# The first matmul group behind a layer norm, issued chunk by chunk over four banks

## The chip, the cores and the metric

The kernel runs on one core of a Trainium2 chip. The metric is the device time of one execution in microseconds (us). The kernel before took 1475.57 us, the median of three runs from 1472.57 to 1479.77. Its profiled execution is a run of its own and took 1484.27 us.

## The reference, cut to what matters

One inference step of a decoder trunk with two layers, on 256 prompt tokens and 8 sample tokens (264 columns in the kernel), width 1024. In each layer a SwiGLU FFN, a token mixer and a second SwiGLU FFN follow one another, with a layer norm behind each:

```python
def swiglu(x, wg, wu, wd):
    return (jax.nn.silu(x @ wg) * (x @ wu)) @ wd

def decoder_layer(x, pos, lp, past):
    x = layer_norm(ALPHA * x + 0.5 * swiglu(x, lp['ffn_wg'][0], lp['ffn_wu'][0], lp['ffn_wd'][0]), lp['ln_g'][0], lp['ln_b'][0])
    y, st = token_mixing(x, pos, lp, past)
    x = layer_norm(ALPHA * x + y, lp['ln_g'][1], lp['ln_b'][1])
    x = layer_norm(ALPHA * x + 0.5 * swiglu(x, lp['ffn_wg'][1], lp['ffn_wu'][1], lp['ffn_wd'][1]), lp['ln_g'][2], lp['ln_b'][2])
    return x, st
```

So the work is one chain: six norms, and behind each but the last a product of the norm's whole output with new weights. The mixer begins with h @ w_in, whose columns feed three head groups; one of them also compresses old keys and values from cache pages (nsa_compress).

## The kernel before, in words

x lies with features on the partitions, in KC = 8 chunks of 128 x 264. A product in full precision is made of three matmuls on halves: every operand is split into a rounded high part and the low rest, and `product` (L713) issues low weight with high x (L715), high weight with low x (L716) and high weight with high x (L717). All are 128x128 weights on 264 columns, or on 512 columns in the mixer's projection.

An FFN's first part runs over 11 groups of weights of 256 hidden columns, gate and up, in three slots. Per group PE does two halves q, and for each a gate bank and an up bank with eight chunks of three matmuls: 96 matmuls on banks 0 to 3. Group n+1 reuses the banks of group n and waits for hidden_done, the multiplication on VectorE (DVE, L1522) that empties them behind the silu on ScalarE (ACT, L1195). In each group ACT splits the next group's weights (w_high, L1189, two halves), and DVE takes the rest of them (w_low, L1436), one half ahead of each silu and multiplication.

A norm ends like this: ACT writes x (L1168) and x_high or mix_x_high (L1170) per chunk; DVE writes the low part (L1418, or L1499 for the mixer) per chunk; the first bank of the next product waits for the low part of its chunk.

In the rows below the five places behind norms 0 to 4 are called M0 (mixer, first layer, near 230 us), F1 and F2 (FFN, near 530 and 742 us), M3 (mixer, second layer, near 954 us) and F3 (FFN, near 1253 us).

The mixer's product starts with four banks of 24 matmuls, whose readers are the convolution on DVE and the gelu on ACT, and goes on with four groups of three tiles on 512 columns (the projection). Between the tiles PE also compresses cache pages: `compress` (L637) needs a set of pages in bc_pages that SyncE's queue (SP, L435, four loads a set) has brought and DVE has weighted (L1581). There are two buffers; a set is loaded into one when the compression two sets earlier is done (bc_used). All orders are written out by hand, and each engine goes through its own list in order.

## Time and profile before

| | us |
|---|---|
| median of three runs | 1475.57 |
| profiled execution | 1484.27 |
| its span, first to last instruction | 1482.5 |
| TensorE busy | 1321.7 |
| VectorE busy | 815.5 |
| ScalarE busy | 516.0 |

The profile is of one execution. TensorE is the engine with most work, and the chain that ended last runs over it for 78% of the span. The mean clock granted to it is 0.926 of its full 2.4 GHz; it has two levels, full and half. Busy times overlap between engines, so what a stage costs is read from what its waits end on.

### The profile page before, as it was taken

The page shows a single profiled execution, that of the slowest core. Times are in us where ns is not written, and L with a number is a line of the kernel's source. Part 1 is how long each engine was busy: PE and PEld are TensorE (multiplying, and loading weights), DVE is VectorE, ACT ScalarE, POOL GpSimd, SP SyncE. Part 2 cuts the span into 40 slices and gives each one's busy share as a digit, 9 for nine tenths or more (in the row PEclk, how much of TensorE's full clock was granted, in tenths as well). Part 3 has the DMA queues.
Part 4 walks back from the last instruction along what each step waited for, and adds up shares of the span by engine and source line. Part 5 has one row for each costly group of instructions (what it writes and reads, how often), then busy time and mean ns, then how long its engine had stood idle before and what let it go on. Part 6 is the DMA issues. An engine that isn't in the chain of part 4 may idle for free.

```text
span 1482.5 us, 24841 instructions
## 1 busy us (share of the span) xinstructions
PE 1321.7 (89%) x9864; PEld 1165.0 (79%) x9864; DVE 815.5 (55%) x1548; ACT 516.0 (35%) x760; POOL 94.5 (6%) x160
## 2 busy tenths in 40 slices
PE   6999997996788979999899999798968787999994
PEld 5999996555565779999799999765646566999993
DVE  5565548764554365554465553678444653665433
ACT  3433335301334254333353333532122433434331
POOL 9000001001000010000110000100100001000001
PEclk9999998997679989999989999899867999999997
DMA  7654574457154235545635556544741713454530
GB/s 256 208 186 136 157 225 141 154 155 248 51 149 117 77 114 171 172 154 176 209 118 171 170 157 179 179 143 149 247 153 32 197 57 114 155 187 153 157 118 30
DMA packets 254824, 226.75 MB, mean 153 GB/s; under 512 B 12596, under 2 KB 234946, under 8 KB 254594
## 3 DMA queue, kind: packets, MB, share of 16 engines
q1 hardware_dynamic: 250530, 220.79, 47.3%
q0 software_dynamic: 4192, 4.56, 0.9%
q8 instruction: 69, 1.13, 0.3%
q14 instruction: 33, 0.27, 0.1%
HBM read 221.44 MB, written 3.86 MB: 152 GB/s over the span
## 4 chain that ended last, share of the span: by engine, by line
PE 78%; DVE 10%; SPq 3%; ACT 3%; issue 3%; DMA 2%; POOL 0%; DVEq 0%; ACTq 0%
PE bank L715 21%; PE bank L717 21%; PE bank L716 21%; PE bank L637 5%; PE bank L878 3%; PE bank L928 2%; SPq L403 1%; PE bank L724 1%; SPq L412 1%; PE bank L725 1%; DMA ring<-in_cache_a_kv_dram 1%; ACT x L1168 1%; DVE rstd L1737 1%; PE bank L1070 1%; PE bank L978 1%
## 5 line engine op out<-in xcount | busy, mean ns | idle before, releaser
L715 PE MATMUL bank<-x_high,w_low 128*128 128x264 f32 x1408 | 406.6, 289 | 28.4 <-DVE x_low L1418 24.4
L716 PE MATMUL bank<-x_low,w_high 128*128 128x264 f32 x1408 | 403.6, 287 | 0.0
L717 PE MATMUL bank<-x_high,w_high 128*128 128x264 f32 x1408 | 403.4, 287 | 0.0
L1436 DVE TENSOR_TENSOR w_low<-weights,w_high 128x2048 fp32r<-128x2048 f32 (+1 forms) x172 | 347.7, 2039 | 68.8 <-ACT w_high L1147 53.7
L715 PEld LDWEIGHTS bank<-x_high,w_low 128*128 128x128 f32 x1408 | 269.7, 192 | 32.3 <-issue 27.9
L716 PEld LDWEIGHTS bank<-x_low,w_high 128*128 128x128 f32 x1408 | 270.4, 192 | 0.0
L717 PEld LDWEIGHTS bank<-x_high,w_high 128*128 128x128 f32 x1408 | 268.8, 191 | 0.0
L715 PE MATMUL bank<-hidden_high,w_low 128*128 128x264 f32 x704 | 205.0, 291 | 0.0
L717 PE MATMUL bank<-hidden_high,w_high 128*128 128x264 f32 x704 | 199.9, 284 | 0.0
L716 PE MATMUL bank<-hidden_low,w_high 128*128 128x264 f32 x704 | 198.9, 283 | 0.0
L1189 ACT ACTIVATE w_high<-weights 128x2048 fp32r<-128x2048 f32 (+1 forms) x88 | 163.8, 1861 | 6.2 <-DMA weights<-in_ffn_wu_dram 6.1
L1522 DVE TENSOR_TENSOR shared<-shared,bank 128x264 f32<-128x264 f32 x88 | 37.8, 429 | 192.5 <-PE bank L717 192.5
L1195 ACT ACTIVATE shared<-bank 128x264 f32<-128x264 f32 x88 | 34.4, 391 | 300.8 <-PE bank L717 300.8
L1147 ACT ACTIVATE w_high<-weights 128x1408 fp32r<-128x1408 f32 (+1 forms) x84 | 125.6, 1543 | 28.9 <-DMA weights<-in_w_in_dram 28.9
L715 PEld LDWEIGHTS bank<-hidden_high,w_low 128*128 128x128 f32 x704 | 132.5, 188 | 0.8
L716 PEld LDWEIGHTS bank<-hidden_low,w_high 128*128 128x128 f32 x704 | 132.4, 188 | 0.8
L717 PEld LDWEIGHTS bank<-hidden_high,w_high 128*128 128x128 f32 x704 | 132.6, 188 | 0.0
L561 POOL TENSOR_TENSOR z<-z,mean_sb 128x264 f32<-128x264 f32 x45 | 36.6, 846 | 1158.2 <-DVE mean_sb L1472 1158.2
L1157 ACT ACTIVATE ring<-z 128x264 f32<-128x264 f32 x48 | 20.3, 424 | 248.0 <-DVE z L1470 248.0
L1470 DVE SCALAR_TENSOR_TENSOR z<-bank,x 128x264 f32<-128x264 f32 x48 | 20.7, 432 | 149.2 <-PE bank L717 105.6
L715 PE MATMUL bank<-w_high,mix_x_low 128*128 128x512 f32 (+1 forms) x192 | 78.7, 410 | 0.0
L716 PE MATMUL bank<-w_low,mix_x_high 128*128 128x512 f32 (+1 forms) x192 | 77.0, 401 | 0.0
(307 smaller groups left out, 1733.1 us busy)
## 6 DMA issues: line engine op xcount, KB each, us to landing
weights<-in_ffn_wg_dram SPq DMA_DIRECT2D x44, 1024.0 KB, 5.1
weights<-in_ffn_wu_dram SPq DMA_DIRECT2D x44, 1024.0 KB, 7.4
weights<-in_ffn_wd_dram SPq DMA_DIRECT2D x64, 704.0 KB, 5.8
weights<-in_w_in_dram SPq DMA_DIRECT2D x20, 1024.0 KB, 5.1
bc_pages<-in_cache_bc_kv_dram SPq DMA_DIRECT2D x128, 128.0 KB, 2.1
ring<-in_cache_bs_kv_dram SPq DMA_DIRECT2D x96, 128.0 KB, 2.2
ring<-in_cache_bw_kv_dram SPq DMA_DIRECT2D x12, 512.0 KB, 4.0
weights<-in_cache_bs_kv_dram SPq DMA_DIRECT2D x32, 128.0 KB, 3.6
```

Of the source, the lines that this page charges most:

```text
L561: nc.gpsimd.tensor_tensor(z[:, c, :], z[:, c, :], mean_sb[:, :], ALU.subtract).then_inc(sub_done, 1)
L637: return mm(*a, skip_group_check=True, **k)
L715: mm(out, w_low, v_high, start=start, stop=False)
L716: mm(out, w_high, v_low, start=False, stop=False)
L717: return mm(out, w_high, v_high, start=False, stop=stop)
L878: last = mm(out, w[:, c, (g % 4) * P:(g % 4 + 1) * P], mixed[:, c, :], start=(c == 0), stop=(c == KC - 1))
L928: last = nc.tensor.transpose(out[:, j * P:(j + 1) * P], tile, ident)
L1147: go(high(k, half), raw(k, half), ACT.Copy).then_inc(high_done, 1)
L1189: go(high(k, q), raw(k, q), ACT.Copy).then_inc(high_done, 1)
L1195: go(silu[:, q, :], banks[2 * q][:, 0:TOK], ACT.Silu).then_inc(silu_done, 1)
L1436: tt(low(k, half), raw(k, half), high(k, half).bitcast(F32), ALU.subtract).then_inc(low_done, 1)
L1522: tt(h, h, banks[2 * q + 1][:, 0:TOK], ALU.mult).then_inc(hidden_done, 1)
```

## The change

In the FFNs behind a norm (all but the first of the program) the first group is issued by a new function `opening`: the chunks are the outer loop, the four banks the inner one. `product` takes its matmuls in another order, so that the one with x_low comes last, and can be told to wait ahead of that one. The mixer's first four banks are issued in the same way, and their three compressions stand together behind them. For the mixer's norms ACT writes mix_x_high ahead of x, and DVE's low part waits for both. In the first group of these FFNs ACT splits both halves of the next weights ahead of the two silus, and DVE both low halves ahead of the two multiplications.

```diff
@@ -674,14 +674,36 @@
                                 pe.wait_ge(low_done, done + (i + 1))
                             wh, wl = (w(k, i).rearrange("p (c f) -> p c f", c=KC) for w in (high, low))
                             for c in range(KC):
-                                if isinstance(n0, int) and n0 + q + i == 0:
+                                if f == 0 and isinstance(n0, int) and n0 + q + i == 0:
                                     pe.wait_ge(low_x_ready, (3 * l + 2 * j) * KC + c + 1)
                                 last = product(banks[2 * q + i][:, 0:TOK], wh[:, c, q * P:(q + 1) * P],
                                                wl[:, c, q * P:(q + 1) * P], x_high[:, c, :], x_low[:, c, :],
                                                c == 0, c == KC - 1)
                             last.then_inc(full, 1)
 
-                for g in range(SLOTS):
+                def opening(k):
+
+                    pe.wait_ge(hidden_done, f * FC)
+                    pe.wait_ge(low_done, halves_before(l, k) + 2)
+                    halves = [[w(k, i).rearrange("p (c f) -> p c f", c=KC) for w in (high, low)] for i in range(2)]
+                    n = 3 * l + 2 * j - 1
+                    for c in range(KC):
+                        pe.wait_ge(high_x_ready, n * KC + c + 1)
+                        low_ready = (low_x_ready, (n + 1) * KC + c + 1)
+                        for q in range(2):
+                            for (wh, wl), full in zip(halves, (gate_full, up_full)):
+                                last = product(banks[2 * q + (full is up_full)][:, 0:TOK], wh[:, c, q * P:(q + 1) * P],
+                                               wl[:, c, q * P:(q + 1) * P], x_high[:, c, :], x_low[:, c, :],
+                                               c == 0, c == KC - 1, low_ready)
+                                low_ready = None
+                                if c == KC - 1:
+                                    last.then_inc(full, 1)
+
+                if f:
+                    opening(base)
+                else:
+                    group(base, halves_before(l, base), 0)
+                for g in range(1, SLOTS):
                     group(base + g, halves_before(l, base + g), 2 * g)
                 with pe.Fori(1, LOOPED) as i:
                     for s in range(SLOTS):
@@ -709,12 +731,13 @@
 
                 residual(3 * l + 2 * j, down)
 
-            def product(out, w_high, w_low, v_high, v_low, start, stop):
-
+            def product(out, w_high, w_low, v_high, v_low, start, stop, low_ready=None):
 
                 mm(out, w_low, v_high, start=start, stop=False)
-                mm(out, w_high, v_low, start=False, stop=False)
-                return mm(out, w_high, v_high, start=False, stop=stop)
+                mm(out, w_high, v_high, start=False, stop=False)
+                if low_ready is not None:
+                    pe.wait_ge(*low_ready)
+                return mm(out, w_high, v_low, start=False, stop=stop)
 
             def residual(n, y_chunk):
 
@@ -757,16 +780,17 @@
 
 
                 k = WIN_USE
-                for m in range(4):
-                    out = bank_v() if m < 2 else bank_a()
-                    for c in range(KC):
-                        if m == 0:
-                            pe.wait_ge(low_x_ready, (3 * l + 1) * KC + c + 1)
-                        last = product(out[:, 0:TOK], *parts_of(k, c, slice(m * P, (m + 1) * P)),
-                                       mix_x_high[:, c, :], mix_x_low[:, c, :], c == 0, c == KC - 1)
-                    last.then_inc(v_full if m < 2 else a_full, 1)
-                    if m:
-                        compress()
+                outs_f = [bank_v(), bank_v(), bank_a(), bank_a()]
+                for c in range(KC):
+                    pe.wait_ge(high_x_ready, 3 * l * KC + c + 1)
+                    for m in range(4):
+                        last = product(outs_f[m][:, 0:TOK], *parts_of(k, c, slice(m * P, (m + 1) * P)),
+                                       mix_x_high[:, c, :], mix_x_low[:, c, :], c == 0, c == KC - 1,
+                                       None if m else (low_x_ready, (3 * l + 1) * KC + c + 1))
+                        if c == KC - 1:
+                            last.then_inc(v_full if m < 2 else a_full, 1)
+                for m in range(3):
+                    compress()
 
                 for g in range(4):
                     k = WIN_USE + 1 + g
@@ -1165,9 +1189,11 @@
                     act.wait_ge(norm_done, n * KC + c + 1)
                     affine = dict(bias=params[:, l, 24 + i * 8 + c:25 + i * 8 + c],
                                   scale=params[:, l, i * 8 + c:i * 8 + c + 1])
+                    if i == 0:
+                        go(mix_x_high[:, c, :], z[:, c, :], ACT.Identity, **affine).then_inc(high_x_ready, 1)
                     go(x[:, c, :], z[:, c, :], ACT.Identity, **affine).then_inc(x_ready, 1)
-                    if split_x(n):
-                        go((x_high if i else mix_x_high)[:, c, :], z[:, c, :], ACT.Identity, **affine).then_inc(high_x_ready, 1)
+                    if i and split_x(n):
+                        go(x_high[:, c, :], z[:, c, :], ACT.Identity, **affine).then_inc(high_x_ready, 1)
                 if i != 0 and n < 3 * DEPTH - 1:
 
                     go(warm[:, :], warm[:, :], ACT.Silu)
@@ -1182,11 +1208,15 @@
                 def group(g, i=None):
 
                     k = base + g + 1
+                    value = landed_value(l, k)
+                    act.wait_ge(landed[k % SLOTS], value if i is None else i * 32 + value)
+                    opened = f and g == 0 and i is None
+                    if opened:
+                        for q in range(2):
+                            go(high(k, q), raw(k, q), ACT.Copy).then_inc(high_done, 1)
                     for q in range(2):
-                        if q == 0:
-                            value = landed_value(l, k)
-                            act.wait_ge(landed[k % SLOTS], value if i is None else i * 32 + value)
-                        go(high(k, q), raw(k, q), ACT.Copy).then_inc(high_done, 1)
+                        if not opened:
+                            go(high(k, q), raw(k, q), ACT.Copy).then_inc(high_done, 1)
                         n = f * FC + 2 * g + q
                         act.wait_ge(gate_full, n + 1 if i is None else i * (2 * SLOTS) + (n + 1))
                         if i is not None or n >= 2:
@@ -1493,6 +1523,7 @@
             def low_of_norm(n, c):
 
                 dve.wait_ge(high_x_ready, n * KC + c + 1)
+                dve.wait_ge(x_ready, (n + 1) * KC + c + 1)
                 if n % 3:
                     low_x(c)
                 else:
@@ -1507,8 +1538,12 @@
 
                 def group(g, i=None):
 
+                    opened = f and g == 0 and i is None
+                    if opened:
+                        split_low(l, base + g + 1)
                     for q in range(2):
-                        split_low(l, base + g + 1, (q,), i)
+                        if not opened:
+                            split_low(l, base + g + 1, (q,), i)
                         n = 2 * g + q
                         value = f * FC + n + 1
                         if i is not None:
```

PE, at the start of the FFN behind norm 1; L715 to L717 are the three matmuls of a product. Before:

```order
L715 MATMUL bank<-x_high,w_low 128x264 [waits low_done,low_x_ready,hidden_done,v_free]
L716 MATMUL bank<-x_low,w_high 128x264
L717 MATMUL bank<-x_high,w_high 128x264
L715 MATMUL bank<-x_high,w_low 128x264 [waits low_x_ready]
L716 MATMUL bank<-x_low,w_high 128x264
L717 MATMUL bank<-x_high,w_high 128x264
```

After, with L736, L737 and L740 in their place:

```order
L736 MATMUL bank<-x_high,w_low 128x264 [waits low_done,high_x_ready,hidden_done,v_free]
L737 MATMUL bank<-x_high,w_high 128x264
L740 MATMUL bank<-x_low,w_high 128x264 [waits low_x_ready]
L736 MATMUL bank<-x_high,w_low 128x264
L737 MATMUL bank<-x_high,w_high 128x264
L740 MATMUL bank<-x_low,w_high 128x264
L736 MATMUL bank<-x_high,w_low 128x264
L737 MATMUL bank<-x_high,w_high 128x264
```

The wait for x_low moved from the first matmul of a chunk to the third, and further banks follow before the next chunk.

PE, in the mixer behind norm 0, around the compressions (L637). Before, the end of the second bank, the first compression and the third bank's start:

```order
L716 MATMUL bank<-mix_x_low,w_high 128x264
L717 MATMUL bank<-mix_x_high,w_high 128x264
L637 MATMUL bank<-bc_pages,consts 32x256 [waits bc_weighted]
L637 MATMUL bank<-bc_pages,consts 32x256 x3
L715 MATMUL bank<-mix_x_high,w_low 128x264 [waits low_done]
```

After, the end of the four banks, and then the projection's first matmuls:

```order
L740 MATMUL bank<-mix_x_low,w_high 128x264
L637 MATMUL bank<-bc_pages,consts 32x256 [waits bc_weighted]
L637 MATMUL bank<-bc_pages,consts 32x256 x3
L637 MATMUL bank<-bc_pages,consts 32x256 [waits bc_weighted]
L637 MATMUL bank<-bc_pages,consts 32x256 x3
L637 MATMUL bank<-bc_pages,consts 32x256 [waits bc_weighted]
L637 MATMUL bank<-bc_pages,consts 32x256 x3
L736 MATMUL bank<-w_high,mix_x_low 128x512 [waits low_done,v_free]
L737 MATMUL bank<-w_high,mix_x_high 128x512
```

The three compressions, which had 24 matmuls between them, now stand side by side ahead of the projection.

DVE, in the first group of the FFN behind norm 1: w_low is the low half of weights, L1522 the multiplication. Before:

```order
L1436 TENSOR_TENSOR w_low<-weights,w_high 128x2048 [waits high_done,states_stored,rows_stored]
L1522 TENSOR_TENSOR shared<-shared,bank 128x264 [waits up_full,silu_done]
L1524 CAST hidden_high<-shared 128x264 [waits hidden_done]
L1526 TENSOR_TENSOR hidden_low<-shared,hidden_high 128x264 [waits hidden_high_done]
L1436 TENSOR_TENSOR w_low<-weights,w_high 128x2048 [waits high_done]
L1522 TENSOR_TENSOR shared<-shared,bank 128x264 [waits up_full,silu_done]
```

After, with L1466 for the split and L1557 for the multiplication:

```order
L1466 TENSOR_TENSOR w_low<-weights,w_high 128x2048 [waits high_done,states_stored,rows_stored]
L1466 TENSOR_TENSOR w_low<-weights,w_high 128x2048 [waits high_done]
L1557 TENSOR_TENSOR shared<-shared,bank 128x264 [waits up_full,silu_done]
L1559 CAST hidden_high<-shared 128x264 [waits hidden_done]
L1561 TENSOR_TENSOR hidden_low<-shared,hidden_high 128x264 [waits hidden_high_done]
L1557 TENSOR_TENSOR shared<-shared,bank 128x264 [waits up_full,silu_done]
```

The second half's split moved ahead of the first multiplication.

## Rows read from the trace of the kernel before

**Rows 1.** The page: the span, and the busy time of each engine.

```profile
span 1482.5 us, 24841 instructions
...
PE 1321.7 (89%) x9864; PEld 1165.0 (79%) x9864; DVE 815.5 (55%) x1548; ACT 516.0 (35%) x760; POOL 94.5 (6%) x160
```

**Rows 2.** PE's waits: us in total, times, longest us.

```profile
PE bank L715 <- DVE x_low L1418: 24.4, 8, 7.5
PE bank L715 <- issue: 19.1, 3, 7.5
```

**Rows 3.** Timeline of ACT at F1: start us, us, instruction [idle before].

```profile
527.65 0.61 ACT L1168 ACTIVATE x<-z,params 128x264 f32<-128x264 f32 x1 [2.56 <-DVE z L1486]
...
535.17 0.59 ACT L1170 ACTIVATE x_high<-z,params 128x264 fp32r<-128x264 f32 x1
535.78 1.28 ACT L1173 ACT_TABLE_LOAD   x1
...
537.18 1.89 ACT L1189 ACTIVATE w_high<-weights 128x2048 fp32r<-128x2048 f32 x1
```

**Rows 4.** Timeline of DVE at F1.

```profile
529.31 0.97 DVE L1418 TENSOR_TENSOR x_low<-x,x_high 128x264 fp32r<-128x264 f32 x1
...
539.21 2.29 DVE L1436 TENSOR_TENSOR w_low<-weights,w_high 128x2048 fp32r<-128x2048 f32 x1 [2.98 <-ACT w_high L1189]
541.47 0.43 DVE L1522 TENSOR_TENSOR shared<-shared,bank 128x264 f32<-128x264 f32 x1
```

**Rows 5.** Timeline of PE at F1.

```profile
530.43 0.56 PE L715 MATMUL bank<-x_high,w_low 128*128 128x264 f32 x1 [7.54 <-DVE x_low L1418]
...
536.63 0.39 PE L717 MATMUL bank<-x_high,w_high 128*128 128x264 f32 x1
536.82 0.42 PE L715 MATMUL bank<-x_high,w_low 128*128 128x264 f32 x1
...
540.10 0.29 PE L715 MATMUL bank<-x_high,w_low 128*128 128x264 f32 x1
540.23 0.29 PE L716 MATMUL bank<-x_low,w_high 128*128 128x264 f32 x1
```

**Rows 6.** Stretches: us, busy us of each engine (instructions), PEclk, DMA, GB/s.

```profile
530.40:547.10 16.70, 15.57 (x97) 14.79 (x98) 9.98 (x17) 12.92 (x18) 0.00 (x0) 0.81 0.00 1
...
742.20:758.90 16.70, 16.69 (x97) 15.70 (x98) 10.00 (x17) 12.90 (x18) 3.67 (x8) 0.72 0.03 9
...
954.00:972.90 18.90, 18.88 (x121) 16.25 (x121) 14.21 (x27) 11.20 (x17) 0.00 (x0) 0.75 0.18 53
...
1252.80:1268.00 15.20, 14.54 (x98) 13.69 (x99) 9.92 (x17) 12.92 (x18) 0.00 (x0) 0.87 0.00 1
310.50:313.40 2.90, 0.00 (x0) 0.00 (x1) 2.68 (x8) 0.00 (x0) 0.00 (x0) 1.00 0.55 150
313.40:318.20 4.80, 4.80 (x20) 3.48 (x21) 1.49 (x2) 0.00 (x0) 2.05 (x4) 0.64 0.65 189
```

**Rows 7.** Timelines of PE, SP and DVE at M0.

```profile
241.12 0.64 PE L637 MATMUL bank<-bc_pages,consts 128*32 128x256 f32 x8
...
248.47 0.64 PE L637 MATMUL bank<-bc_pages,consts 128*32 128x256 f32 x8
...
241.96 10.18 SPq L435 DMA_DIRECT2D bc_pages<-in_cache_bc_kv_dram  x12
...
246.07 1.22 DVE L1581 TENSOR_TENSOR bc_pages<-bc_pages,cmp_w 128x1024 f32<-128x1024 f32 x1 [2.26 <-DMA bc_pages<-in_cache_bc_kv_dram]
```

**Rows 8.** Timelines of PE and DVE at M3.

```profile
964.91 0.64 PE L637 MATMUL bank<-bc_pages,consts 128*32 128x256 f32 x8
...
972.26 0.64 PE L637 MATMUL bank<-bc_pages,consts 128*32 128x256 f32 x8
...
970.71 1.23 DVE L1581 TENSOR_TENSOR bc_pages<-bc_pages,cmp_w 128x1024 f32<-128x1024 f32 x1 [3.20 <-DMA bc_pages<-in_cache_bc_kv_dram]
```

**Rows 9.** The page: DMA issues, KB each, us to landing.

```profile
bc_pages<-in_cache_bc_kv_dram SPq DMA_DIRECT2D x128, 128.0 KB, 2.1
```

## The prediction

> **What bounds the kernel now.** I read the page first. The tensor engine (PE) is busy for 1321.7 of 1482.5 us [rows 1], so a gain has to come out of its idle stretches or out of the clock it is granted. Next I read the list of what PE waits for. Two lines concern the matmuls on a norm's output: 24.4 us for x_low and 19.1 us put down to "issue", the longest of both 7.5 us [rows 2]. There are five such places, one behind each norm but the last. I call them F1, F2, F3 (the norm hands over to an FFN; near 530, 742 and 1253 us) and M0, M3 (to the mixer; near 230 and 954 us). The timelines of ACT, DVE and PE at F1 show the handover. ACT makes x and x_high chunk by chunk, about 1.0 us per chunk, from 527.65 to 535.76, loads a table and starts on the next weights at 537.18 [rows 3]. DVE makes x_low(0) at 529.31 [rows 4]. PE starts at 530.43, and until 536.63 it has done only 24 matmuls, since its first bank takes three per chunk; then the other 72 of the group run freely [rows 5].
>
> The second thing to see is the clock. Fifteen matmuls from 536.82 to 540.10 go by at 0.219 us each; from 540.10 on one takes 0.12 us [rows 5]: 1.2 GHz and 2.4 GHz. The table by stretches gives the share granted. From a share s over a length L the time at half speed is 2(1-s)L, and half of that is lost: F1 6.3 us (3.2 lost), F2 9.4 (4.7), F3 4.0 (2.0), M3 9.5 (4.7) [rows 6]. The clock is low because PE had just been idle for 7.5 us. After 2.9 us of idleness, from 310.5 to 313.4, the next 4.8 us also had a share of only 0.64 [rows 6], so a wait of 3 us suffices.
>
> **The change, part by part.**
>
> *Opening of an FFN.* The same 96 matmuls are issued in another order: twelve per chunk on four banks. Only the third of the twelve needs x_low first, and the later chunks arrive every 1.0 us while twelve matmuls take 12 x 0.12 = 1.45 us or 12 x 0.219 = 2.6 us. So PE never waits again after x_low(0). Two of the 96 are done before it. The other 94 take, with h us at half speed, h + (94 - h/0.219) x 0.12 = 11.3 + 0.45h. For h under gapless work I take 4 us (F3's 4.0 and the 3.5 behind 313.4 [rows 6]), with 2.8 to 6.3 as bounds: 13.1 us (12.5 to 14.1), so F1 would end at 530.4 + 13.1 = 543.5.
>
> What is late next is DVE. PE's second group reuses the first two banks, and waits until the multiplication that empties them is done. In the old order the banks were full 48 matmuls earlier, and this was hidden. Now the four banks get full within the last 12 matmuls, and DVE has put both low halves ahead of that multiplication. Its chain from ACT: first w_high starts at 537.18, DVE's first w_low at 539.21, its end at 541.47 [rows 3, 4]; the second adds 2.26 (543.7) and the multiplication 0.43 and some 0.1 for the handover: 544.3. That is later than 543.5, and sets the start of group two. Before it was 547.1, so -2.8 at F1. The same 13.9 us behind the first matmul gives 756.1 instead of 758.9 at F2 (-2.8), and 1266.7 instead of 1268.0 at F3 (-1.3) [rows 6]. PE idles for about 0.8 us in there; that is less than the 2.9 above, and I charge no loss of clock. Splitting both halves first costs ACT nothing: it had been ahead of PE anyway. Group two itself has its weights split by then, and what it frees, it frees earlier.
>
> *Opening of the mixer.* Here the order also moves three compressions (L637). They stood behind the second, third and fourth bank; now all three stand behind the last matmul. bc_pages has two buffers. The third compression needs a set of pages which SP may load only when the first compression is done, and which DVE then weights. The rows of M0: first compression 241.12 to 241.76, loads issued from 241.96, DVE starts at 246.07 and needs 1.22, so 5.5 us from the one's end to the other's start. At M3 964.91 + 0.64 to 970.71 + 1.23: 6.4 us [rows 7, 8]. In between PE had 48 matmuls and a compression; now it has one compression of 0.6 us. So a new wait of about 4.9 and 5.8 us stands in PE's queue, and behind it the whole projection. Working M3 out: opening 954.0 + 13.1 = 967.1, first compression 0.64, reload 6.4, third 0.64: 974.8, against 972.26 + 0.64 = 972.9 before: +1.9. At M0 the reload is 0.9 shorter: +1.0. The wait is longer than the 2.9 us that lowered the clock, so the projection starts at half speed; with the 4 us from above that loses 2.0 (1.4 to 3.2). Together +3.0 and +3.9. x_high ahead of x (norms 0 and 3) lets two matmuls go earlier and leaves x_low where it was: nothing. The later product order issues as many matmuls and weight loads as before: nothing. DVE's additional wait is for an x that ACT wrote just ahead of, or 0.5 us behind, x_high: nothing.
>
> The Trainium skill speaks against this piece. "DMA: Bandwidth & Descriptors", section Rules for kernel authors, tells to issue a DMA early, compute, and wait late, since the fixed cost then overlaps; the moved compressions take that computing away. The same page (Anatomy of one DMA) fits the fixed cost at about 2.0 us on the GpSimd path. Estimated by that page a reload would be 2.0 + 1.2 = 3.2 us, and the sum would be 5.5 us lower; the rows of this kernel say 5.5 and 6.4, and I go by them.
>
> **Sum.** Against the profiled execution (1484.27 us, of which 1482.5 is span): -2.8 - 2.8 - 1.3 + 3.0 + 3.9 = 0. But that execution is 8.7 us above the median of the runs (1475.57), and in four of five openings its clock came late. In an execution where it comes as early as at F3, the old opening loses less while the new one, bound by DVE or by the reload, gains nothing from it. So for the runs I take F nearer F3: -1.7 each (between -1.0 and -2.8), -5.1 in all. For M an early clock gives the old opening up to (9.5 - 4.0)/2 = 2.8 back, so between +3.0 and +6.7; I take +4.8 each, +9.6. Net +4.5: 1480.
>
> **Rivals.**
> 1. *The half clock behind the reload lasts.* In the projection PE shares its time with waits for bc_pages, so the clock may need as long as at M3 and F2 (9.5 us, 4.7 lost) instead of 4. For: four of five openings show 6 us and more. Against: the projection's matmuls come gapless. It adds 2.7 to each M: +4.5 + 5.4 = +9.9, 1485.5, slower. It decides from about 6.9 us at half speed on.
> 2. *The reload is quick.* The list of DMA issues has 2.1 us from issue to landing for one load of bc_pages [rows 9]; if the four of a set overlapped, the reload would be 2.1 + 1.2 = 3.3, the wait 2.7 us, below the one that lowered the clock. Each M then falls by 2.2 to 3.1 and by the 2.0 of clock: +0.1 each at most, -5 to -8 in all with the F: 1469, the side of faster. Against: 4.1 us in M0's own rows.
> 3. *The delay is absorbed.* Later in the mixer PE waits for caches. If those loads were not held up by the compressions, the M would cost nothing: -5, 1470.5. Against: SP issues the caches behind the page loads in one queue.
> 4. *Changing banks costs.* The Trainium skill's "TensorE: Matmul & The Clock Gate", section A second HAM failure mode, tells of micro-idles when a kernel cycles through banks, which lower the clock. As a mechanism here: all 94 matmuls at 0.219 = 20.6 us, F +4 each, M +7.5 more each, about +35: 1510. Against: the one bank change in the rows, 536.63 to 536.82, has a step of 0.19, no gap [rows 5].
>
> **Chances.** Forecast 0.58 (within 0.5% 0.50, slower 0.08), rival 1 0.22 (slower 0.20, within 0.02), rival 2 0.13 (faster 0.08, within 0.05), rival 3 0.05 (faster 0.02, within 0.03), rival 4 0.02 (slower). A measurement of this kernel can tell about 0.5% (7.4 us) from no change. That makes faster 0.10, same 0.60, slower 0.30. The bounds: F 3 x (-2.8 to -1.0) and M 2 x (+3.0 to +6.7) give -2.4 to +10.4; the runs scatter by 3 to 4 us; so 1471 to 1488.
>
> **What would show it.** Right: at F1 to F3 no wait of PE between x_low(0) and the end of the opening; DVE's second w_low ending after PE's opening, with PE idle for up to 1 us; group two 13.9 us behind the first matmul that needs x_low. In the mixer: PE idle 5 to 6 us ahead of the third compression, released by DVE's weighting, and a share of 0.5 behind it. Wrong: a third compression without a wait (rivals 2, 3), gaps inside the opening (rival 4), or a second group that starts at PE's own pace.

## The result, and the profile after

The changed kernel takes 1482.40 us (median of 20 runs, 1474.73 to 1490.76), the kernel before 1477.81 (20 runs, 1469.01 to 1484.46). The ratio is 1.0045, with a 95% interval from 1.0027 to 1.0063: slower by 4 to 9 us (6.7 by the ratio; the medians are 4.6 apart). The profiled execution has a span of 1481.0 us, against 1482.5 in [rows 1]; as single executions scatter by more than the change, the stages have to be read one by one.

The page of the changed kernel, the lines that answer to [rows 1]:

```profile
span 1481.0 us, 24880 instructions
...
PE 1312.8 (89%) x9864; PEld 1159.1 (78%) x9864; DVE 815.1 (55%) x1548; ACT 516.6 (35%) x760; POOL 94.8 (6%) x160
```

What PE of the changed kernel waits for (us in total, times, longest), answering to [rows 2]:

```profile
PE bank L637 <- DVE bc_pages L1616: 20.6, 8, 5.2
PE bank L736 <- ACT x_high L1196: 18.0, 3, 6.0
...
PE bank L736 <- ACT mix_x_high L1193: 11.3, 2, 5.6
```

The 7.5 us behind each norm became 6.0 and 5.6, and they end on the high half now. The compressions' waits for bc_pages are 20.6 us in eight now, the longest 5.2. Both are what the change does by its order; what they are worth is in the timelines.

PE at F1 in the changed kernel, where [rows 5] stood:

```profile
527.75 0.56 PE L736 MATMUL bank<-x_high,w_low 128*128 128x264 f32 x1 [6.01 <-ACT x_high L1196]
528.10 0.42 PE L737 MATMUL bank<-x_high,w_high 128*128 128x264 f32 x1
529.20 0.59 PE L740 MATMUL bank<-x_low,w_high 128*128 128x264 f32 x1 [0.68 <-DVE x_low L1448]
...
542.34 0.28 PE L740 MATMUL bank<-x_low,w_high 128*128 128x264 f32 x1
542.97 0.39 PE L736 MATMUL bank<-x_high,w_low 128*128 128x264 f32 x1 [0.35 <-DVE shared L1557]
```

DVE there, where [rows 4] stood:

```profile
538.08 4.49 DVE L1466 TENSOR_TENSOR w_low<-weights,w_high 128x2048 fp32r<-128x2048 f32 x2 [2.99 <-ACT w_high L1216]
542.49 0.42 DVE L1557 TENSOR_TENSOR shared<-shared,bank 128x264 f32<-128x264 f32 x1
```

From the first matmul on x_low to group two PE takes 13.8 us (529.20 to 542.97), without a gap until the last, and the row at 542.97 names DVE's multiplication, which follows the two splits at once.

PE at M0 in the changed kernel, where [rows 7] stood:

```profile
244.47 1.07 PE L637 MATMUL bank<-bc_pages,consts 128*32 128x256 f32 x16
250.74 1.08 PE L637 MATMUL bank<-bc_pages,consts 128*32 128x256 f32 x8 [5.20 <-DVE bc_pages L1616]
```

The first row is two compressions, the second the third one: it waits 5.2 us, and itself takes 1.08 us, where a compression took 0.64. The reload of its set, on SP's queue and on DVE:

```profile
245.31 10.14 SPq L435 DMA_DIRECT2D bc_pages<-in_cache_bc_kv_dram  x12
...
249.46 1.23 DVE L1616 TENSOR_TENSOR bc_pages<-bc_pages,cmp_w 128x1024 f32<-128x1024 f32 x1 [4.89 <-DMA bc_pages<-in_cache_bc_kv_dram]
```

The set's four loads are the first of the twelve in SP's row. In the trace SP issues them one after another, from 245.31 to 247.47, and the last lands at 249.43, 2.0 us behind its issue; DVE, idle for 4.9 us, starts at once.

The changed kernel by stretches (columns as in [rows 6]): projection's first tile at M0 and M3, and the openings F1, F2 and F3 from the first matmul on x_low:

```profile
251.80:259.70 7.90, 7.90 (x27) 6.02 (x24) 5.03 (x14) 0.00 (x0) 0.00 (x0) 0.70 0.59 187
529.20:543.00 13.80, 13.44 (x95) 13.24 (x95) 9.32 (x16) 11.62 (x18) 0.00 (x0) 0.86 0.01 1
738.40:752.10 13.70, 12.94 (x94) 12.73 (x94) 9.22 (x15) 11.95 (x18) 3.72 (x8) 0.90 0.04 11
...
968.80:976.60 7.80, 7.80 (x28) 5.96 (x24) 5.11 (x15) 0.00 (x0) 0.00 (x0) 0.71 0.61 202
1252.60:1266.40 13.80, 13.53 (x95) 13.32 (x95) 9.32 (x16) 11.53 (x18) 0.00 (x0) 0.85 0.01 1
```

The three FFN openings take 13.7 to 13.8 us, where 16.7, 16.7 and 15.2 stood (counted there from the first matmul, which waited for the first x_low). The projection's first tile of 24 matmuls takes 7.8 to 7.9 us with a share of 0.70 and 0.71.

The clock falls a second time later in the mixer. The seventh tile, from the seventh compression to the eighth, at M0, in the kernel before and in the changed one:

```profile
277.57:283.88 6.31, 6.31 (x32) 4.58 (x32) 4.86 (x7) 2.10 (x4) 0.00 (x0) 1.00 0.32 88
...
282.52:290.43 7.91, 7.91 (x32) 5.74 (x32) 4.87 (x7) 2.10 (x4) 0.00 (x0) 0.78 0.42 115
```

To compare places across kernels I count from the start of DVE's copy of a norm's mean. "Group three" is the 193rd matmul of an FFN, "first tile done" the start of the fourth compression, "twelfth compression done" the start of the matmul behind it.

| us behind the mean | before | changed | FFN part alone | mixer part alone | compressions inside | all three moves | filled norms |
|---|---|---|---|---|---|---|---|
| M0 projection starts | 26.4 | 28.9 | 24.9 | 28.9 | 25.1 | 23.2 | 22.5 |
| M0 first tile done | 32.1 | 36.9 | 30.6 | 36.8 | 31.0 | 29.4 | 29.5 |
| M3 first tile done | 32.0 | 36.6 | 30.6 | 36.6 | 30.7 | 29.1 | 28.9 |
| M0 twelfth compression done | 87.4 | 93.8 | 85.9 | 93.7 | 86.3 | 86.3 | 86.3 |
| M3 twelfth compression done | 87.4 | 93.4 | 85.9 | 93.5 | 86.0 | 84.4 | 84.2 |
| F1 group two | 24.1 | 21.2 | 21.5 | 24.1 | 21.2 | 21.7 | 19.0 |
| F1 group three | 35.7 | 32.9 | 33.3 | 35.7 | 32.9 | 33.5 | 30.8 |
| F2 group three | 35.8 | 32.9 | 32.9 | 35.5 | 32.9 | 32.8 | 32.4 |
| F3 group three | 34.1 | 32.9 | 32.9 | 34.1 | 33.7 | 33.4 | 30.8 |

In the two traces the FFNs give back 2.8, 2.9 and 1.2 us. The mixers cost 4.8 and 4.6 up to the end of the first tile, and 6.4 and 6.1 up to the end of the twelfth compression, since the seventh tile takes 7.9 us instead of 6.3 or 6.4. A wait of 1.7 us for bc_pages stands ahead of that tile in all 24 mixers of the twelve kernels traced here, the kernel before among them. The clock falls behind it in all six in which PE stood idle for 5.2 to 5.3 us ahead of the third compression (changed kernel, mixer part alone, x first), and in two of the 18 others (M0 of all three moves and of the filled norms). Why it falls there is open. Further on single executions differ by more than this: from one norm's mean to the next M0's mixer takes 300.3 us before and 299.0 after, M3's 298.7 and 305.1.

### The profile page after: what moved, and what is told of

Its sections match the earlier page's. It is cut to its first block, busy times and chain, and to the rows that moved or that the text cites. A ratio compares the mean times of both kernels' runs of the same rounds, so it can differ in the third digit from the quotient of the medians.

```text
span 1481.0 us, 24880 instructions
## 1 busy us (share of the span) xinstructions
PE 1312.8 (89%) x9864; PEld 1159.1 (78%) x9864; DVE 815.1 (55%) x1548; ACT 516.6 (35%) x760; POOL 94.8 (6%) x160
## 4 chain that ended last, share of the span: by engine, by line
PE 75%; DVE 11%; ACT 5%; SPq 4%; issue 2%; DMA 2%; POOL 0%; DVEq 0%; ACTq 0%
PE bank L736 20%; PE bank L737 20%; PE bank L740 20%; PE bank L637 5%; PE bank L902 3%; PE bank L952 2%; SPq L403 2%; DVE w_low L1466 1%; PE bank L747 1%; SPq L412 1%; PE bank L748 1%; DMA ring<-in_cache_a_kv_dram 1%; ACT x L1194 1%; PE bank L937 1%; ACT x_high L1196 1%
## 5 line engine op out<-in xcount | busy, mean ns | idle before, releaser
L736 PE MATMUL bank<-x_high,w_low 128*128 128x264 f32 x1408 | 404.1, 287 | 23.5 <-ACT x_high L1196 18.0
L740 PE MATMUL bank<-x_low,w_high 128*128 128x264 f32 x1408 | 402.5, 286 | 2.0 <-DVE x_low L1448 2.0
L737 PE MATMUL bank<-x_high,w_high 128*128 128x264 f32 x1408 | 402.5, 286 | 0.0
L1466 DVE TENSOR_TENSOR w_low<-weights,w_high 128x2048 fp32r<-128x2048 f32 (+1 forms) x172 | 347.5, 2039 | 69.5 <-ACT w_high L1171 53.8
L736 PEld LDWEIGHTS bank<-x_high,w_low 128*128 128x128 f32 x1408 | 268.9, 191 | 25.3 <-issue 23.3
L740 PEld LDWEIGHTS bank<-x_low,w_high 128*128 128x128 f32 x1408 | 267.5, 190 | 3.0 <-DVE x_low L1448 3.0
L737 PEld LDWEIGHTS bank<-x_high,w_high 128*128 128x128 f32 x1408 | 269.1, 191 | 0.0
L736 PE MATMUL bank<-hidden_high,w_low 128*128 128x264 f32 x704 | 204.1, 290 | 0.0
L737 PE MATMUL bank<-hidden_high,w_high 128*128 128x264 f32 x704 | 200.5, 285 | 0.0
L740 PE MATMUL bank<-hidden_low,w_high 128*128 128x264 f32 x704 | 200.0, 284 | 0.0
L1219 ACT ACTIVATE w_high<-weights 128x2048 fp32r<-128x2048 f32 (+1 forms) x82 | 152.4, 1858 | 6.8 <-DMA weights<-in_ffn_wu_dram 6.7
L1557 DVE TENSOR_TENSOR shared<-shared,bank 128x264 f32<-128x264 f32 x88 | 37.7, 428 | 185.6 <-PE bank L740 185.6
L736 PEld LDWEIGHTS bank<-hidden_high,w_low 128*128 128x128 f32 x704 | 132.8, 189 | 0.8
L737 PEld LDWEIGHTS bank<-hidden_high,w_high 128*128 128x128 f32 x704 | 132.3, 188 | 0.8
L740 PEld LDWEIGHTS bank<-hidden_low,w_high 128*128 128x128 f32 x704 | 132.3, 188 | 0.0
L736 PE MATMUL bank<-w_high,mix_x_low 128*128 128x512 f32 (+1 forms) x192 | 82.1, 428 | 0.0
L737 PE MATMUL bank<-w_high,mix_x_high 128*128 128x512 f32 (+1 forms) x192 | 80.0, 417 | 0.0
```

Source lines behind the costliest of these rows:

```text
L736: mm(out, w_low, v_high, start=start, stop=False)
L737: mm(out, w_high, v_high, start=False, stop=False)
L740: return mm(out, w_high, v_low, start=False, stop=stop)
L1219: go(high(k, q), raw(k, q), ACT.Copy).then_inc(high_done, 1)
L1466: tt(low(k, half), raw(k, half), high(k, half).bitcast(F32), ALU.subtract).then_inc(low_done, 1)
L1557: tt(h, h, banks[2 * q + 1][:, 0:TOK], ALU.mult).then_inc(hidden_done, 1)
```

## The experiments

**FFN part alone.** The mixer's opening goes back to bank by bank:

```diff
-                for c in range(KC):
-                    pe.wait_ge(high_x_ready, 3 * l * KC + c + 1)
-                    for m in range(4):
-                        ...
-                for m in range(3):
-                    compress()
+                for m in range(4):
+                    for c in range(KC):
+                        ...
+                    if m:
+                        compress()
```

> The changed kernel with the mixer's first four banks in the old order again (bank by bank, a compression behind each of the last three); the FFN openings stay as changed. My theory (the FFN openings gain, the mixer's loses more): no wait of 5 us ahead of the third compression, 249.1 - 230.1 = 19 us again from the first matmul on x_low to the projection, group two of the FFNs still 13.8 us behind the first matmul on x_low. Time 5 us under the kernel before (ratio 0.9966, between 0.994 and 0.999). Rival (the FFN openings do not matter, or cost): ratio 1.000 or above. Rival (the loss lies in the FFN openings): ratio 1.004, like the whole change.

Measured: 1470.73 us, ratio 0.9952 (0.9928 to 0.9975), 7 us under the kernel before. The long wait for bc_pages is gone, and the FFNs keep their gain (2.4, 2.9 and 1.2 us up to group three). Not all of the 7 us need be theirs: in this trace the mixers are 1.5 us shorter than before too, as the clock rose earlier in their opening (at M0 a share of 0.88 from 229.6 to 246.6 us, against 0.75 from 230.5 to 249.1 before). The rivals, that the FFN openings do not matter or cost, fall.

**Mixer part alone.** PE's `opening` is not called (ACT and DVE split no half ahead either, which is not shown):

```diff
-                if f:
-                    opening(base)
-                else:
-                    group(base, halves_before(l, base), 0)
+                group(base, halves_before(l, base), 0)
```

> The changed kernel with the first group of the FFNs in the old order again, and the weights' halves split one by one; the mixer's opening stays as changed. My theory: the wait of 5.2 us ahead of the third compression and the half clock behind it stay, nothing is gained at the FFNs: 9 to 10 us over the kernel before (ratio 1.006, between 1.003 and 1.009). Rival (the mixer's wait is absorbed later by the waits for caches): ratio 1.000. Rival (the loss lies in the FFNs): ratio 1.000 or below.

Measured: 1489.01 us, ratio 1.0082 (1.0050 to 1.0113), 12 us over the kernel before by the ratio, 11 by the medians. PE at M0 of this version:

```profile
244.15 1.07 PE L637 MATMUL bank<-bc_pages,consts 128*32 128x256 f32 x16
250.47 1.08 PE L637 MATMUL bank<-bc_pages,consts 128*32 128x256 f32 x8 [5.25 <-DVE bc_pages L1613]
```

The same wait as in the whole change, and no later wait absorbs it: by the end of the twelfth compression M0 is 6.3 and M3 6.1 us behind the kernel before. By the ratios the two parts, -7.1 and +12.1, add up to +5.0, and the whole measured +6.7; by the medians -7.2 and +11.1 make +4.0, and the whole +4.6. That fits within the intervals.

**Compressions inside the opening.** The first behind the fourth chunk, the second behind the sixth, the third at the end:

```diff
+                    if c in (3, 5):
+                        compress()
-                for m in range(3):
-                    compress()
+                compress()
```

> The changed kernel with the first compression behind the fourth chunk of the mixer's opening, the second behind the sixth, the third behind the last; all else as changed. My theory: the reload of 5.5 to 6.4 us now runs beside the last four chunks, the wait ahead of the third compression falls from 5.2 us to under 1, the clock stays at full speed into the projection: each mixer gains 5 to 8 us on the changed kernel, total 10 to 15 us under it and 5 to 10 us under the kernel before (ratio 0.994 to 0.997). Rival (the wait is not the reload, but DVE's order of work): the wait stays at 4 us or more, ratio 1.004.

Measured: 1465.94 us, ratio 0.9935 (0.9908 to 0.9962). PE's compressions at M0:

```profile
238.79 0.64 PE L637 MATMUL bank<-bc_pages,consts 128*32 128x256 f32 x8
...
242.47 0.64 PE L637 MATMUL bank<-bc_pages,consts 128*32 128x256 f32 x8
...
247.40 0.64 PE L637 MATMUL bank<-bc_pages,consts 128*32 128x256 f32 x8 [1.21 <-DVE bc_pages L1617]
```

DVE at the same place:

```profile
245.15 0.42 DVE L1626 COPY shared<-bank 128x256 f32<-128x256 f32 x1 [2.00 <-PE bank L740]
...
246.12 1.22 DVE L1617 TENSOR_TENSOR bc_pages<-bc_pages,cmp_w 128x1024 f32<-128x1024 f32 x1
```

The wait fell from 5.2 to 1.2 us. What is left is the rival's share: DVE copies the first banks before it weights the third set, and these copies wait for the opening's end. The reload itself is hidden, and the loss has become a gain: up to the end of the twelfth compression each mixer is 7.4 to 7.5 us shorter than in the changed kernel. The ratio is a little better than the range expected.

**Filling the wait.** Between the second and the third compression, in the changed kernel:

```diff
                 for m in range(3):
+                    if m == 2:
+                        for _ in range(11):
+                            mm(banks[5][:, 0:256], mean_w, consts[:, 0:256], start=True, stop=True, skip_group_check=True)
                     compress()
```

> The changed kernel with 11 matmuls that nobody reads (fp32, 256 columns, some 0.45 us each, 4.9 us in all) between the second and the third compression, into a bank that is free there; they fill the wait of 5.2 us without shortening it. If the half clock behind the wait is a cost of its own (my theory): the share granted stays 1.0 from the opening's rise into the projection, the projection's first tile is 2 to 3 us shorter, 4 to 6 us under the changed kernel in all (ratio to the kernel before 1.000 to 1.002). If the wait alone is the cost (rival): no shorter than the changed kernel, ratio 1.0045.

Measured: 1477.60 us, ratio 1.0003 (0.9977 to 1.0029). Its stretches at M0, from the first compression to the projection, and the first tile:

```profile
243.20:251.20 8.00, 6.53 (x47) 4.64 (x46) 1.86 (x5) 5.35 (x5) 0.00 (x0) 1.00 0.45 123
251.20:257.20 6.00, 5.88 (x32) 4.47 (x30) 5.63 (x16) 0.00 (x0) 0.00 (x0) 1.00 0.61 170
```

The clock stays at 1.00 and the first tile takes 5.9 us, although the third compression starts no sooner (28.7 and 28.0 us behind the mean, in the changed kernel 27.9 and 27.8). The second fall is gone too. So the half clock is a cost of its own: 1.7 and 2.1 us up to the end of the first tile, 3.3 and 3.6 up to the end of the twelfth compression, about half of the loss. Its interval just touches that of the whole change, so it is the two shares, 0.70 and 1.00, and the tile's 7.9 and 5.9 us that show it more than the time.

**All three moves.** The version with the compressions inside, and on DVE the first multiplication back between the two low halves, and the third weighting ahead of the copies:

```diff
-                    opened = f and g == 0 and i is None
-                    if opened:
-                        split_low(l, base + g + 1)
                     for q in range(2):
-                        if not opened:
-                            split_low(l, base + g + 1, (q,), i)
+                        split_low(l, base + g + 1, (q,), i)
                 ...
+                weight()
                 for c in range(2):
                     ...
-                weight()
```

> The version with the compressions inside the mixer's opening, and two more moves on DVE: in the FFNs' first group the second low half stands behind the first multiplication again (ACT still splits both halves ahead of the silus), and in the mixer the third set of pages is weighted ahead of the copies that wait for the opening's end. My theory: DVE's second split is what holds group two of the FFNs, so it now starts within 0.6 us of the end of the opening, 0.5 to 1 us earlier at each; the 1.2 us wait ahead of the third compression is DVE's order and goes. In all 3 to 5 us less than the version with the compressions inside alone, ratio to the kernel before 0.991. Rival: the split is needed for the up bank of group two, whose wait takes what is gained: no difference at the FFNs, ratio 0.992 to 0.994.

Measured: 1467.41 us, ratio 0.9946 (0.9922 to 0.9971), not to be told from the compressions inside alone. In the trace both mixers are 1.6 us shorter again up to the first tile's end, and the third compression does not wait; at M0 the second fall of the clock takes this back. The FFNs are not shorter: group two follows the opening without a gap, but two of the openings (F1, F2) took longer, since the clock rose later. The time did not bear out the 3 to 5 us.

**Halves one by one.** The version with the compressions inside, and ACT and DVE in the old order beside PE's new opening, a single run. On ACT, and on DVE as in the version above:

```diff
-                    opened = f and g == 0 and i is None
+                    opened = False
```

> The version with the compressions inside the opening, but ACT and DVE split the next weights' halves one by one again, as in the kernel before, while PE keeps the new opening. My theory: the second high half then waits behind the first silu for the end of the opening, the second low half behind it, and PE waits for it in the up bank of group two: a gap of 1 to 2 us inside group two, group three starts 0.5 to 1.5 us later than 32.9 us behind the norm's mean. Rival (splitting ahead is not needed): no gap, group three at 32.9 us or earlier.

PE at F1 of this version, the only gap inside group two:

```profile
544.27 0.39 PE L736 MATMUL bank<-x_high,w_low 128*128 128x264 f32 x1 [0.48 <-DVE w_low L1467]
```

PE waits for the second low half, as expected, though for 0.5 us and not 1 to 2. At F2 and F3 the wait is 0.5 us too. Group two takes 12.5 us at all three FFNs, in the version above, which differs on ACT alone in the FFNs, 11.8: splitting ahead on ACT is worth 0.6 to 0.7 us. Group three starts at 33.4, 34.2 and 34.0 us, 0.5 to 1.3 later than in the changed kernel, but the rest of that is the opening, which ended 0.2 to 1.4 us later here. The single run's 1470.33 us says nothing at this size.

**Filling the norms of the kernel before.** Behind the statistics of five norms:

```diff
                 stats(KC - 1)
+                if n < 3 * DEPTH - 1:
+                    for _ in range(16):
+                        mm(banks[5][:, 0:256], mean_w, consts[:, 0:256], start=True, stop=True, skip_group_check=True)
```

> The kernel before with 16 matmuls that nobody reads (fp32, 256 columns, some 0.43 us each, 6.9 us in all) behind the statistics of each of the first five norms, in a stretch in which PE was idle for 7.5 us; nothing is shortened by them. If the half clock at the openings costs what the table by stretches says (my theory): the share granted stays 1.0 through the norms, each opening is 1.5 to 3 us shorter, the mixers' 4 us, 12 us in all: ratio 0.990 to 0.994. If the openings are bound by the order of their work and not by the clock (rival): ratio 0.999 to 1.001.

Measured: 1473.24 us, ratio 1.0007 (0.9990 to 1.0024): no change, which is the rival's forecast and not mine. The stretches F1 and F2, from the first matmul on x_low to group two:

```profile
521.20:537.50 16.30, 14.83 (x97) 13.36 (x97) 9.71 (x17) 12.71 (x18) 0.00 (x0) 0.90 0.00 1
732.90:747.70 14.80, 13.32 (x96) 11.86 (x96) 9.70 (x16) 12.69 (x18) 3.48 (x7) 1.00 0.03 10
```

With a full clock F2 took 15.0 us from its first matmul (732.70 to 747.72) instead of 16.7, and at F1 the clock fell in the middle all the same. In the old opening the first bank goes at the pace at which ACT and DVE hand over the chunks: at F2 it takes 6.3 us at full clock (732.70 to 739.02) with waits of up to 0.37 us for x_low, and 6.7 us at half clock in the kernel before (742.21 to 748.89). Most of the gain is in the other three banks. In this trace F2 and M3 start their next stage 1.6 and 1.5 us earlier than in the profiled execution before, M0, F1 and F3 within 0.1 us of it.

**Filled norms.** All three moves, the first two compressions behind the fifth and seventh chunk, and 12 such matmuls behind each of the five norms:

```diff
+                if n < 3 * DEPTH - 1:
+                    for _ in range(12):
+                        mm(banks[5][:, 0:256], ...)
-                    if c in (3, 5):
+                    if c in (4, 6):
```

> The version with all three moves, the first two compressions behind the fifth and seventh chunk, and 12 matmuls that nobody reads behind each of the first five norms (5.2 us of the 5.6 to 6.0 in which PE is idle there). My theory: the openings run at full speed, 94 matmuls in 11.5 us; group two of the FFNs starts near 19.5 us behind the mean instead of 21.2, the mixers' projection near 21.5 instead of 25: 8 to 13 us under the version without the filling, ratio to the kernel before 0.982 to 0.987. Rival (DVE's splits bound the FFNs whatever the clock): the FFNs unchanged, the mixers alone gain, ratio 0.987 to 0.990.

Measured: 1460.81 us, ratio 0.9915 (0.9887 to 0.9943). By the median this is the fastest version, 14 us under the kernel before in the same series and 6.6 under all three moves; the intervals of the three versions with the compressions inside overlap. The gain over the version without the filling is under the 8 to 13 us expected. F1, from the first matmul on x_low to group two:

```profile
525.10:536.70 11.60, 11.59 (x95) 11.51 (x95) 7.11 (x15) 11.14 (x17) 0.00 (x0) 1.00 0.01 1
```

95 matmuls in 11.6 us at F1, and F3 is like it; at F2 the clock fell once and group two started at 20.6 us. The mixers gained less than expected: the tile ahead of the fourth compression now ends in a wait of 1.2 us for that compression's pages, and at M0 the clock fell again in the seventh tile (7.9 us).

**Filled norms, halves split ahead.** The same, with both low halves ahead of the first multiplication again, a single run:

```diff
+                    opened = f and g == 0 and i is None
+                    if opened:
+                        split_low(l, base + g + 1)
                     for q in range(2):
-                        split_low(l, base + g + 1, (q,), i)
+                        if not opened:
+                            split_low(l, base + g + 1, (q,), i)
```

> The version with the filled norms, with DVE's two low halves ahead of the first multiplication again, as in the changed kernel. My theory: with PE at full speed the opening ends 19 us behind the mean, but the multiplication cannot begin before 20.7 us, so group two starts at 21.2 us at all three FFNs whatever the clock, with PE idle for 2 us; the version with the multiplication between the halves started it at 19.0. Rival (DVE does not decide): group two at 19.0 again.

DVE at F1 of this version:

```profile
527.45 4.49 DVE L1470 TENSOR_TENSOR w_low<-weights,w_high 128x2048 fp32r<-128x2048 f32 x2 [2.99 <-ACT w_high L1220]
531.87 0.42 DVE L1561 TENSOR_TENSOR shared<-shared,bank 128x264 f32<-128x264 f32 x1
```

PE's group two there:

```profile
532.34 0.39 PE L736 MATMUL bank<-x_high,w_low 128*128 128x264 f32 x1 [2.06 <-DVE shared L1561]
```

Group two starts at 21.2 us at all three FFNs. PE is idle for 2.1 us before it at F1 and F2, and for 0.5 at F3, where the clock fell in the opening (a share of 0.87). Without the split ahead it started at 19.0, 20.6 and 19.0. So DVE's order decides here, and the clock that PE had does not.

**x first.** The changed kernel with x ahead of mix_x_high in the mixers' norms, a single run:

```diff
+                    go(x[:, c, :], z[:, c, :], ACT.Identity, **affine).then_inc(x_ready, 1)
                     ...
-                    go(x[:, c, :], z[:, c, :], ACT.Identity, **affine).then_inc(x_ready, 1)
```

> The changed kernel with ACT writing x ahead of mix_x_high again in the mixers' norms. My theory: the first matmul of the mixer's opening is 0.5 us later, the first one on the low half and all behind it where they were (7.4 us behind the mean, projection at 28.8 to 28.9): no effect on the time. Rival: the opening starts later as a whole, by 0.5 us.

The first matmul moved from 5.6 to 6.1 us behind the mean; the first on x_low (7.4) and the projection (28.7 and 28.8) stayed. The single run's 1487.95 us says nothing at this size.

## Why the prediction was right

The predicted time was 1480.0 with 1471 to 1488; measured were 1482.4. Of the 2.4 us between them 2.2 are the kernel before, whose median of 20 runs is 1477.81 where three runs gave 1475.57. The change itself was put at +4.5 and measured +4.6 by the medians, +6.7 by the ratio. The mechanism was right; that the sum is so near is partly luck, as both of its terms were too small and have opposite signs.

- **The FFN opening** held to its size. Predicted were 13.9 us from the first matmul on x_low to group two, measured 13.7 to 13.8 three times; -2.8, -2.8 and -1.3 against the profiled execution, measured -2.8, -2.9 and -1.2. For the runs I took -5.1; the part alone measured -7.1 (-10.6 to -3.7).
- **What is late next** is DVE, as the step said. The changed kernel's own row names it, and with a full clock the start stays at 21.2 us until the multiplication moves. Where the clock rose later, PE itself was as late: at F1 of the FFN part alone group two starts at 21.5 without a wait.
- **The reload** is the new wait: 5.2 us twice, against 4.9 and 5.8 predicted. Filling it, removing it and the part alone all point to it. Rival 2 (a quick reload) falls: one load lands in 2.0 to 2.2 us, but SP issues the four over 2.2 us, so they overlap only in part. Rival 3 (absorbed later) falls, as the loss is still there at the twelfth compression and in the part's time. The Trainium skill's rule ("DMA: Bandwidth & Descriptors", Rules for kernel authors: issue early, compute, wait late) is borne out by the compressions inside, which is that rule applied. The 2.0 us that the Trainium skill ("DMA: Bandwidth & Descriptors", Anatomy of one DMA) gives for one DMA on the GpSimd path are near what one of these loads takes on SP. The estimate with them was too short, since it left out the time between the issues: DVE starts 4.2 us behind the first (245.31 to 249.46).
- **The mixer's size** was too small against the profiled execution: +3.0 and +3.9 predicted, +4.8 and +4.6 measured at the end of the first tile. The opening took 14.0 to 14.3 us instead of 13.1, as its clock rose later than the 4 us I took; the third compression took 1.08 us instead of 0.64, a term I had left out; and the tile behind it lost 2.1 to 2.2 us instead of 2.0. At M3 the reload was some 0.7 us shorter than I had it. The second fall of the clock, another 1.5 to 1.6 us at each mixer, I had not foreseen at all.
- **The step to the runs** came out for a weak reason. I gave the old mixer's opening up to 2.8 us back for an early clock, from the rule that half of the time at half speed is lost. The filled norms of the kernel before show that this overstates it: 4.7 us were "lost" at F2, and a full clock gave 1.7 back. The +4.8 per mixer that I took is what the first tile shows, but for another reason, and the part alone measured +12.1 for two (+7.4 to +16.7), near the 6.4 and 6.1 of the trace at the twelfth compression.
- **Rival 1** (the half clock behind the reload lasts) did not come in its form: a share of 0.70 over 7.9 us is 4.7 us at half speed, and the clock was full again within 8 us. Part of its price came all the same: the seventh tile, a share of 0.78 over 7.9 us, adds 3.5 us at half speed, together 8.2, above the 6.9 from which it would decide. **Rival 4** (changing banks costs) did not come: with a full clock the opening's 95 matmuls took 11.6 us, PE busy for 11.59 of them.
- **"A wait of 3 us suffices"** was read from one row and does not hold everywhere. In the version with the compressions inside PE waits 2.91 us for bc_pages at M3 (until 1022.93), and the 5 us behind it have a share of 1.00.

## What to carry to other kernels

When a loop is turned inside out, look at everything that was spread over it: the compressions waited for nothing between the banks and for 5 us side by side, because a reload with two buffers ran beside the matmuls. And when all banks fill at the same time, the engine that empties them must not have long work queued ahead; what was 48 matmuls of slack becomes a wait. Here the wait of 5.2 us on PE was paid more than once: as itself, in the tile behind it (2.1 to 2.2 us), and in a tile 30 us later (1.5 to 1.6 us). But a share of half clock is only worth what the stretch would gain from a faster PE.

## What was not expected of the hardware

Matmuls that nobody reads, put where PE had waited for 5.2 us, kept the clock at 1.00, and the tile behind them took 5.9 us instead of 7.9. Behind the norms, with an order of work that can use it, they brought the openings of F1 and F3 from 14.3 and 14.2 us (all three moves without them) to 11.6; in the kernel before they gave no time that can be measured, since its first bank waits for the chunks.
